# Gate tiles of the GLA stage as pairs of seven products, with the order of the forget-gate chain kept

## What is computed

```
u = x @ w_in
u_gate, u_gla, u_rwkv, u_ssm = _split(u, (N_GATE, GLA_PROJ, RWKV_PROJ, SSM_PROJ))
o_gla, s_gla = _gla_mixer(u_gla, ...)
o_rwkv, ... = _rwkv7_mixer(u_rwkv, ...)
o_ssm, ... = _mamba2_mixer(u_ssm, ...)
g = jax.nn.sigmoid(u_gate).reshape(b, l, 3, d)
merged = g[:, :, 0] * (o_gla @ gla_wo) + g[:, :, 1] * (o_rwkv @ rwkv_wo) + g[:, :, 2] * (o_ssm @ ssm_wo)
h = _layer_norm(DN_ALPHA * x + merged @ w_out, ...)
h = _layer_norm(DN_ALPHA * h + _moe(h, ...), ...)
```

## Time and profile before

| what | value |
|---|---|
| median of 3 runs | 1447.16 us (1446.69 to 1448.29) |
| the profiled execution | 1444.06 us, its span 1442.0 us |
| TensorE busy | 1415.1 us, 98% |
| VectorE, ScalarE, GpSimd busy | 724.3, 411.3, 234.9 us |
| GLA stage | from 631.55 to about 745.5 us of the span |
| granted TensorE clock | 0.999 of full speed |

### The profile page before, as it was taken

The page is one execution under the profiler, slowest core; times in us unless marked ns, Lnnn a source line. Parts: engine busy times, 40 slices in busy tenths (PEclk is TensorE's granted clock), DMA queues, the critical chain, the costliest instruction groups (busy, mean ns, idle before and its releaser), DMA issues.

```text
span 1442.0 us, 32350 instructions
## 1 busy us (share of the span) xinstructions
PE 1415.1 (98%) x13523; PEld 1024.3 (71%) x13523; DVE 724.3 (50%) x1360; ACT 411.3 (29%) x847; POOL 234.9 (16%) x193
## 2 busy tenths in 40 slices
PE   7999999999999999999999999999999999999997
PEld 6999777677777777667779985864476766757752
DVE  7443778887754677735458654623311112211217
ACT  2332543443432554434533211111111111111112
POOL 3784113230110111130013000011010000000000
PEclk9999999999999999999999999999999999999999
DMA  7796473744254444566568639699999999999996
GB/s 284 191 197 151 136 214 100 216 167 132 81 136 127 139 136 120 185 184 192 159 231 216 217 116 386 241 407 407 427 425 429 427 427 428 428 427 428 429 408 273
DMA packets 158017, 375.73 MB, mean 261 GB/s; under 512 B 102320, under 2 KB 110944, under 8 KB 139952
## 3 DMA queue, kind: packets, MB, share of 16 engines
q1 hardware_dynamic: 142048, 346.63, 67.2%
q0 software_dynamic: 7152, 16.85, 3.4%
q10 hardware_dynamic: 8672, 10.20, 2.0%
HBM read 329.22 MB, written 51.95 MB: 264 GB/s over the span
## 4 chain that ended last, share of the span: by engine, by line
PE 85%; DVE 6%; DMA 2%; ACT 2%; DVEq 2%; issue 1%; SPq 1%; ACTq 1%
PE PS L733 19%; PE PS L1303 15%; PE PS L1322 8%; PE PS L750 7%; PE PS L1149 6%; PE PS L1270 6%; PE PS L817 3%; PE PS L1129 2%; DVE region L1831 2%; PE PS L1191 2%; PE PS L1275 2%; DVE region L1838 2%; PE PS L1213 1%; DMA region<-projected 1%; PE PS L825 1%
## 5 line engine op out<-in xcount | busy, mean ns | idle before, releaser
L733 PE MATMUL PS<-h0T,region 128*128 128x320 f32 x1360 | 390.2, 439 | 2.0 <-issue 1.7
L1435 ACT ACTIVATE region<-PS 128x320 f32<-128x320 f32 (+5 forms) x351 | 145.7, 426 | 676.8 <-PE PS L733 237.6
L733 PEld LDWEIGHTS PS<-h0T,region 128*128 128x128 f32 x1360 | 251.2, 190 | 111.7 <-issue 15.0
L1303 PE MATMUL PS<-region 128*64 128x512 f32 x1024 | 228.1, 592 | 0.0
L1303 PEld LDWEIGHTS PS<-region 128*64 128x64 f32 x1024 | 117.6, 137 | 101.6 <-issue 49.8
L1831 DVE TENSOR_TENSOR region<-region 128x512 f32<-128x512 f32 (+10 forms) x237 | 165.3, 717 | 34.1 <-DMA region<-expert_rows 5.0
L1435 ACT ACTIVATE region<-region 128x256 f32<-128x256 f32 (+10 forms) x229 | 99.5, 465 | 83.0 <-DVEq L1854 13.7
L1322 PE MATMUL PS<-region,history 128*64 128x512 f32 x512 | 119.2, 597 | 1.1 <-ACTq L1771 0.5
L1831 DVE TENSOR_TENSOR history<-region,PS 128x256 f32<-128x256 f32 x32 | 13.5, 421 | 199.7 <-ACTq L1766 199.7
L1435 ACT ACT_TABLE_LOAD x77 | 98.8, 1283 | 25.3 <-ACTq L1482 9.8
L1838 DVE SCALAR_TENSOR_TENSOR region<-region,feature_vectors 128x320 f32<-128x320 f32 (+1 forms) x103 | 77.2, 750 | 53.2 <-ACTq L1511 41.0
(11 more groups left out here) (250 smaller groups left out, 1576.2 us busy)
## 6 DMA issues: line engine op xcount, KB each, us to landing
region<-moe_w SPq DMA_DIRECT2D x65, 2048.0 KB, 30.3
region<-moe_w SPq DMA_DIRECT2D x65, 1024.0 KB, 29.3
region<-w_in SPq DMA_DIRECT2D x115, 512.0 KB, 5.7
region<-wo SPq DMA_DIRECT2D x32, 512.0 KB, 4.3
expert_rows<-region SPq DMA_DIRECT2D x20, 512.0 KB, 7.2
region<-expert_rows SPq DMA_DIRECT2D x5, 2048.0 KB, 17.3
projected<-region ACTq DMA_DIRECT2D x59, 167.5 KB, 4.0
region<-projected SPq DMA_DIRECT2D x10, 768.0 KB, 6.8
```

The lines of the kernel that those rows point to most:

```text
L733: last = mm(PS[:, 6 + i % 2, 0:NTOK], WR[:, i, k, :], H0T[:, k, :], start=(k == 0), stop=(k == KT - 1))
L1303: last = mm(PS[tiles(i), 2, :], XE[:, k, tiles(i)], W13[r][i][:, k * 512:k * 512 + 512], start=(k == 0), stop=(k == KT - 1))
L1435: return nc.scalar.activation(out, in_, f, **kw)
```

## The change

The 16 gate tiles become eight pairs g = 0 to 7, two to a chunk, with products 1 to 7 in the accumulators X (bank 6), Z and W (the halves of bank 7). All pairs share these. Chunk c has products 1 to 6 of pair 2c behind the decay product, product 7 and products 1 to 5 of pair 2c+1 behind the values, and 6 and 7 behind the state's sums. In chunk 0, products 1 and 2 stand ahead of the wait for the rows. ScalarE copies products 1, 2, 3 and 5 (`keep_gate`); VectorE makes three adds (`gate_first`, and twice `gate_rest`); GpSimd adds the weights (`gate_sums`), with the merge's token sums between. SP stores the tiles instead of ScalarE. Bias and absolute value of the next chunk (`gate_decays`) close VectorE's chunk, which is where they stood before. GpSimd saves the token sums in `GTOK` during SSM chunk 0. Core of the diff:

```
 TensorE, gla(c)
+                if c == 0:
+                    gate_pair(0, 1, 2)
...
                 last.then_inc(sem("gl_pre"), 1)
+                if c is not NPC:
+                    gate_pair(2 * c, 1 if c > 0 else 3, 6)
...
                 last.then_inc(sem("gl_v"), 1)
-                for f in range(3):
-                    fill(f)
+                if c is not NPC:
+                    gate_pair(2 * c, 7, 7)
+                    gate_pair(2 * c + 1, 1, 5)
...
                 last.then_inc(sem("state_sums"), 1)
-                fill(3)
+                if c is not NPC:
+                    gate_pair(2 * c + 1, 6, 7)
 TensorE, gate_pair: waits ahead of the products
+                    if k == 1:
+                        for m, i in ((n, a), (n + 1, b)):
+                            pe.wait_ge(sem(f"weights_in{i}"), (m // RING + 1) * 16)
+                        if g > 0:
+                            pe.wait_ge(sem("added_out"), 3 * g - 1)
+                        else:
+                            pe.wait_ge(sem("tile_moved"), N_GLA + 2)
...
+                    if k == 3:
+                        pe.wait_ge(sem("weights_summed"), p + 1)
+                        pe.wait_ge(sem("quad_kept"), 4 * p + 1)
...
+                    if k == 6:
+                        pe.wait_ge(sem("quad_kept"), 4 * p + 3)
...
+                    if k == 7:
+                        pe.wait_ge(sem("quad_kept"), 4 * p + 4)
+                        pe.wait_ge(sem("added_out"), 3 * g + 1)
 VectorE, gla(c)
+                if pairs:
+                    gate_first(2 * c)
+                    gate_rest(2 * c)
                 dve.wait_ge(sem("softplus_out"), NCH + one)
...
                 dve.drain().then_inc(sem("gl_ops"), 1)
+                if pairs:
+                    gate_first(2 * c + 1)
...
                 dve.drain().then_inc(sem("gl_state"), 1)
+                if pairs:
+                    gate_rest(2 * c + 1)
...
                 dve.drain().then_inc(sem("gl_out"), 1)
+                if pairs:
+                    gate_decays(c + 1)
 GpSimd
-            for q in (0, 2):
-                token_sums(q)
+            for g in range(GATE_PAIRS):
+                gate_sums(g)
+                if g in (1, 3):
+                    token_sums(g - 1 if g == 3 else 0)
 SP
+            gate_weights(1)
             gla_rows(1)
+            for c in range(NPC - 1):
+                gate_weights(2 * c + 2)
+                gate_stores(2 * c)
+                gate_weights(2 * c + 3)
+                gla_rows(c + 2)
+                gate_stores(2 * c + 1)
```

More of the change, by code:

```diff
@@ L39 @@
 UNITS = 12
+GATE_PAIRS = 8
 UNIT_ORDER = (0, 2, 3, 1)
@@ L245, in hybrid_layer @@
         UAS = (UA, UA2)
+        at[0] = mixer_end + 24 * L
+        GKEPT = take(4, NTOK // 2)
+        gates_at = 31872
+        assert at[0] <= 27776 and ssm_end <= gates_at
+        at[0] = gates_at
+        GTOK = take(4, KT // 2, NTOK // 2)
+        GSUM = [take(4, KT // 2, 128) for _ in range(2)]
+        assert at[0] <= 36864 + 768 + KT * 128
         at[0] = mixer_base
@@ L553, in _ @@
             sp.dma_start(io['out_ssm'][1], SN).then_inc(sem("state_out"), 16)
-            weights((N_GLA - 1) // RING, (N_GLA - 1) % RING)
+            for n in range(N_GLA - 1, N_GLA + 2):
+                weights(n // RING, n % RING)
             sp.wait_ge(sem("phase_over"), ENG * 3)
@@ L567, in gla_rows, with gate_weights, gate_stores @@
                 sp.dma_start(UGS[c % 2], ut[T_GLA:T_GLA + 24, :, c, HIST:CW].rearrange("t p w -> p t w")).then_inc(sem(landed), 16)
[L569 to L571 removed]
+            def gate_weights(g):
+                n = gate_tiles(g)[0]
+                for m in (n, n + 1):
+                    weights(m // RING, m % RING)
+            def gate_stores(g):
+                n, a, b = gate_tiles(g)
+                sp.wait_ge(sem("added_out"), 3 * g + 3)
+                for m, i in ((n, a), (n + 1, b)):
+                    sp.dma_start(ut[TILE[m], :, :, :], STG[:, i, :, :]).then_inc(sem(f"store_done{i}"), 16)
             def gla_out(s):
@@ L1660, in _, with keep_gate @@
                 move(n // RING, n % RING)
+            def keep_gate(g, made, x):
+                act.wait_ge(sem("quad"), 7 * (PAIRS + g) + made)
+                a_(GKEPT[:, x].rearrange("p (c w) -> p c w", c=NCH), tuple(gate_blocks())[(0, 0, 1, 2)[x]], ACT.Copy)
+                act.drain().then_inc(sem("quad_kept"), 1)
             def gla(c):
-                def fill(f):
-                    if c is not NPC:
-                        move(c * (FILL_G // RING) + (N_GLA + f) // RING, (N_GLA + f) % RING)
-                one = c + 1
+                one, pairs = c + 1, c is not NPC
                 act.wait_ge(sem(gla_in(c)[0]), gla_in(c)[1])
                 UG = UGS[c % 2]
+                if pairs:
+                    keep_gate(2 * c, 1, 0)
+                    keep_gate(2 * c, 2, 2)
+                act.wait_ge(sem("softplus_in"), NCH + one)
+                a_(LB4, AB4, ACT.Exp, scale=-1.0)
+                if pairs:
+                    keep_gate(2 * c, 3, 1)
+                if pairs:
+                    keep_gate(2 * c, 5, 3)
+                else:
+                    act.drain()
+                a_(LB4, LB4, ACT.Ln, bias=1.0)
+                act.drain().then_inc(sem("softplus_out"), 1)
                 act.wait_ge(sem("gl_out"), one)
@@ L2323, in gla @@
                 dve.drain().then_inc(sem("gl_out"), 1)
+                if pairs:
+                    gate_decays(c + 1)
+            gate_decays(0)
             for c in range(NPC):
```

114 lines of the change are left out of this document (86 added, 28 removed).

## The result

| | before | changed |
|---|---|---|
| median | 1446.93 us (4 runs, 1444.60 to 1448.29) | 1462.72 us (4 runs, 1459.37 to 1462.98) |
| ratio, 95% interval | | 1.0105 (1.0086 to 1.0125) |
| profiled execution, its span | 1444.06, 1442.0 us | 1462.95, 1461.2 us |

The change costs 1.05% of 1446.93 us, 15.2 us (12.4 to 18.1). The two spans differ by 19.2 us: 0.6 us lie ahead of the GLA stage, 16.0 in it up to chunk 4, and 2.7 behind. That is more than 15.2, in part because the profiled execution of before lay 2.9 us under its median. I compare lengths inside the stage, and the ratios of the two kernels' times with their intervals, which are not exactly the ratios of the medians.

A forecast was written before the change was run, and what follows sets the result against it. TensorE was taken as the bound, with the forget chain 0.2 us behind. Order 0.2 plus GpSimd collisions of 4.0, 5.2, 2.1 and 0.5 gave +12.0 on the 1447.16 us median: 1459.2 us, range 1449.5 to 1465.

The forecast's parts named there:

- order: GLA stage: start and four-engine loop together, without GpSimd collisions, make the kernel 0.2 us slower.
- turns: GLA chunks: VectorE steps with two SBUF operands each wait for a GpSimd operation they meet, 1.3 to 1.5 us.
- heavier rival: GLA stage: the reciprocal waits too and GpSimd's sums come late for product 3; +16 to +20, 1465 us; chance 0.10.
- TensorE's removed work: Gate tiles in the GLA stage: 70.0 us become 60.9 at the projection phase's rate, 9.1 us less, 21.1 a chunk.
- fast rival: GLA stage: shorter loop, TensorE stays the bound, chunks near 21.1 us; 1439.7 us; chance 0.08, with times up to 1444.
- The start: Start of the GLA stage: the first decay product starts 1.6 us later, behind two new products taking 2.17.
- The loop: GLA chunks: in-order copies and adds through four engines make a chunk 24.0 us against 23.4 before, 0.6 slower.
- the 0.6 at product 6: GLA chunk: product 6 needs product 3's copy, queued on ScalarE behind the exponential; 0.6 us more waiting for TensorE.
- +4.0, +5.2, +2.1 and +0.5: Losses to GpSimd collisions in chunks 0, 1, 2 and 3 of the GLA stage, in us.
- The scaling step: Chunk 1's tail: VectorE's scaling, with one SBUF operand, waits for GpSimd; if not, the sum is +10.4, not +12.0.
- The copy of the token sums in the SSM stage: GpSimd's copy of 2560 elements in the SSM stage, up to 4.0 us long: costs nothing, upper end 1 us.
- rival of no turns: GLA stage: GpSimd misses the chain or costs nothing there, only the loop remains; +0.2, 1447.4 us; chance 0.12.

The follow-up runs named there:

- a1: Changed kernel without GpSimd's 32 weight sums, token sums at the start of the stage, order kept; 1450.5 us, ratio 1.0013 to the kernel before.
- r3: Changed kernel with the forget chain ahead of the pairs' copies and additions, without GpSimd's weight sums; 1445.8 us, ratio 0.9990 to the kernel before.
- d1: Changed kernel with 12 spare TensorE matmuls in each of the long waits of chunks 0 and 1; 1458.2 us, ratio 1.0064 to the kernel before.
- c1: Kernel before the change, its order kept, with 32 GpSimd additions of 512 elements added; 1463.2 us, ratio 1.0090 to the kernel before.
- t1: Changed kernel, order kept, with the token sums behind the operands of the last chunk; 1460.3 us, ratio 1.0080 to the kernel before.
- r4: r1 with product 1's copy before the exponential, pair 0's product 2 behind the first forget-gate product, token sums in chunk 4; 1453.8 us, ratio 1.0032.
- r5: r4 with the token sums behind the weight sums of pairs 0 and 1 instead; 1451.3 us, ratio 1.0032 to the kernel before.
- b1: Changed kernel with the token sums behind all weight sums instead of behind those of pairs 1 and 3; 1462.9 us, ratio 1.0094 to the kernel before.
- g1: Changed kernel, order kept, with the token sums behind the weight sums of pairs 0 and 1; 1457.5 us, ratio 1.0065 to the kernel before.
- r1: Changed kernel with the forget chain ahead of the pairs' copies and additions, each chunk's tail moved into the next; 1451.2 us, ratio 1.0021.

## Why the prediction was right

The forecast was 1459.2 us in a range of 1449.5 to 1465, from a sum of +12.0. The result is 1462.7 and +15.2 (12.4 to 18.1). The sum had two parts, order (0.2) and turns (11.8), and a1 separates them. Measured in the stage, its start included, they are 2.2 and 11.2, and 2.6 come from the clock, which had no term: 16.0. The mechanism and its main term were right. But 15.2 lies just above the +8 to +15 that I had called the forecast and gave 0.70: two terms were too small, and none was too large by as much. The upper end of the range had been drawn for the heavier rival, whose turns did not come; that it also covered the clock was luck.

- **TensorE's removed work.** 9.1 us were to go. In the stage itself a pair costs more than in the projection phase: a chunk needs 22.2 us of TensorE (r3), not 21.1, against 23.4 before. The step that failed is carrying the rate of 392 uninterrupted matmuls (784 instructions) into a place where products alternate with the chunk's small matmuls. It made the fast rival too fast: with TensorE the bound, 4 x 1.1 us of its gain weren't there to be had, so by that estimate 1444.1 and not 1439.7.
- **The start.** 1.6 later was forecast. From the last plain group's start to the first decay product it was 14.30 (617.25 to 631.55) and is 16.15, so 1.85.
- **The loop.** 24.0 us a chunk was forecast, a1 has 24.5. Product 3 waits 1.33 to 1.41 (1.3 forecast), L1159 0.7 (0.9), and the 0.6 at product 6 do not show. The remaining half microsecond I put down to TensorE's slower products, which stand in the loop too; no run separates it. Chunk 0 and the start were to come out 1.8 us ahead and are 1.1 ahead, chunks 1 to 3 were to give 1.8 back and give 3.3. So a1's stage is 2.2 us longer than before, against +0.2, and its ratio says 1.9 (0.6 to 3.2).
- **GpSimd's turns.** The terms were +4.0, +5.2, +2.1 and +0.5, in all 11.8. Measured at an even clock, d1 less a1: 24.5 - 20.5 = 4.0, 29.7 - 24.5 = 5.2, 26.0 - 24.6 = 1.4, 25.1 - 24.5 = 0.6, in all 11.2. This is the mechanism, and the step-by-step layout gave its size too, best in chunk 1, where the four steps of the tail lost 4.2 (4.1 forecast). In chunk 0 two parts were off and cancelled: the operands came to their start 1.5 us late (0.9 forecast), and the pair of them lost 2.15 where three operand steps were to lose 3.1. In chunk 2 the sums of pair 6 did not wait for a late landing: they began at 703.04, released by TensorE, met the three scan steps (1.24, 1.60 and 1.27 us) and were over before the operands at 708.76, which kept their 0.43 and 0.76. I had taken them to meet an operand step.
- **The scaling step.** I let it wait (+12.0 and not +10.4). It did: the two scalings take 1.73 together beside the token sums, and 0.61 in a1. The Trainium skill, "SBUF — State Buffer", section "Who interferes with whom", allowed that for a two-port mode. The reciprocal, with one operand, stayed at 1.75 beside GpSimd, so the heavy rival lost its main ground.
- **Left out: the clock.** Two long waits were forecast at their place (4 in chunk 0, 4 in chunk 1; 4.4 and 4.2 measured). That TensorE comes back slower from them was not. It is 2.6 us in the four chunks, from the changed kernel to d1. With the 2.0 by which the order came out dearer, it makes up the distance from 12.0 to the stage's 16.0, less 0.6 for the turns.
- **The merge.** The changed kernel's first merge unit waits 1.61 for VectorE's sums, one of which takes a further turn with GpSimd; the kernel before shows no such wait. The three sums before, then now, and the wait:

```profile
761.63 4.58 DVE L1831 TENSOR_TENSOR region<-region 128x512 f32<-128x512 f32 x3 [0.19 <-issue]
...
779.36 5.83 DVE L1920 TENSOR_TENSOR region<-region 128x512 f32<-128x512 f32 x3 [0.19 <-issue]
...
787.21 3.53 PE L1226 MATMUL PS<-region 128*128 128x160 f32 x24 [1.61 <-DVEq L2486]
```

  The new order alone doesn't bring it: c1, whose merge and order are the old ones, has the same wait of 1.61, and d1, with the new order, has none. All other profiles have it, at 1.60 to 1.90, or 3.87 in t1 and r4. I take it to come and go with small shifts in time; whether the kernel before has it in some executions, no second profile of it shows.
- **The copy of the token sums in the SSM stage.** It was taken at nothing, with up to 1 us. No run separates it, but the last plain group of tiles starts at 617.25 and 618.97 in the two kernels without it and between 616.85 and 621.61 with it, so no more than that spread is in it.

The rival of no turns (0.12) is the one that a1 plays, 1.9 us above before. The faster rival had little ground: even r3, with GpSimd out and a better order, is at 0.9990 (0.9979 to 1.0002).

Not settled: why TensorE is busy 22.5 us in a chunk of r5 and 22.2 in one of r3, the part of d1's gain outside the four chunks, and the 2.7 us behind chunk 4 by which the profile of the changed kernel is longer than that of before, of which the merge's wait is 1.6. No version was found that beats the kernel before.

## What to carry to other kernels

Removed work on the bounding engine pays only down to the next chain: here 0.2 us of slack were on the page before, and the 9.1 us had nowhere to go. Work on an "idle" GpSimd has a price at each VectorE step with two SBUF operands that meets it, here 0.9 to 1.2 us beside GpSimd operations of 1.27 to 1.54, so lay it beside the critical chain step by step, and do the same for every place that it may be moved to: b1, t1 and r4 each moved much of the cost and did not remove it. Take an instruction's rate from a stretch with the same neighbours, and add to a wait of TensorE what its slower clock behind it may cost (1.4 to 1.7 us a time here). Before reading a stage from one profile, look where that execution lies among the others.

## What the runs showed of the hardware that was not expected

TensorE's granted clock can fall to the lower of its two levels (0.50, that is 1.2 of 2.4 GHz) in work that follows a wait. Stretches of 2 us cut out of the traces show these cases:

| run, place | wait ahead, us | lowest clock of a stretch behind it |
|---|---|---|
| b1, chunk 3 | 4.80 | 0.50 |
| changed, chunks 0 and 1 | 4.41, 4.16 | 0.50, 0.50 |
| t1 and r4, merge | 3.87, 3.87 | 0.53, 0.50 |
| c1, chunk 1 | 3.32 | 0.50 |
| g1, chunk 0 | 2.65 | 1.00 |
| b1 and r1, chunk 0; c1, chunk 3 | 2.43, 2.43, 2.39 | 0.56, 0.52, 0.52 |
| r1, chunk 1 | 2.26, and 1.16 a little earlier | 0.50 |
| t1, chunk 0 | 2.01 | 1.00 |
| r1, merge | 1.90 | 0.50 |
| g1, merge | 1.82 | 1.00 |
| r5, chunk 0 | 1.79 | 0.50 |
| changed, merge | 1.61 | 1.00 |

So the length of one wait alone doesn't say whether the clock falls: it fell behind 1.79 and not behind 2.65. d1 shows that work in the gap keeps it up: with 12 spare matmuls in each of the two long gaps it stayed at 1.00.

The turns are not even. In a row of them a GpSimd addition of 512 elements takes 1.45 to 1.55 us in place of 1.27, so it loses 0.2 to 0.3. A VectorE step of 256 elements beside it loses 0.9 to 1.2, most of an addition: in the changed kernel the steps of 0.42, 0.69 and 0.42 take 1.32, 1.87 and 1.54.
